# A mixture-of-experts stage on one core: experts ranked by row count, six of eight run with 96 rows as stationary tiles, eleven weight slots

## The reference

```
def moe_ffn(x, w_router, wg, wu, wd):
    logits = (xf @ w_router)
    top_v, top_i = lax.top_k(logits, 2)
    top_w = softmax(top_v)
    combine = sum(one_hot(top_i, 8) * top_w[..., None], axis=1)
    for e in range(8):
        out = out + combine[:, e:e + 1] * (silu(xf @ wg[e]) * (xf @ wu[e])) @ wd[e]
```

## Time and profile before

| | us |
|---|---|
| three runs | 1996.62, 1998.37, 1999.4 (median 1998.37) |
| profiled execution, its own time | 2003.87 |
| span of the program within it | 2002.0 |
| PE busy / DVE / ACT / POOL | 1873.6 / 375.4 / 248.8 / 137.8 |
| MoE loop, first gate matmul to the copy of the last result | 1030.64 to 1975.71 |

### The profile page before, as it was taken

How to read it: one execution, slowest core, us unless ns; L and a number is a source line. 1 busy time by engine, 2 the same in 40 slices (tenths; PEclk the granted TensorE clock), 3 DMA queues, 4 the chain that set the end, 5 groups by cost and what they waited for, 6 DMA issues and landing times.

```text
span 2002.0 us, 36594 instructions
## 1 busy us (share of the span) xinstructions
PE 1873.6 (94%) x15695; PEld 1515.0 (76%) x15695; DVE 375.4 (19%) x823; ACT 248.8 (12%) x539; POOL 137.8 (7%) x198
## 2 busy tenths in 40 slices
PE   6699999899999999898879999999999999999994
PEld 5489997677776886665679597896969879596982
DVE  2798012100003016564210000000000000000002
ACT  1001001100000115544020000000000000000001
POOL 2053000300000011231010000000000000000001
PEclk9799999899998999999979999999999999999997
DMA  9844655673563626787449799898979989797994
GB/s 243 227 146 147 202 187 203 245 280 126 188 253 127 142 78 266 248 287 221 132 143 296 262 344 300 289 316 273 335 260 343 304 285 321 269 338 262 337 308 150
DMA packets 354325, 484.74 MB, mean 242 GB/s; under 512 B 32612, under 2 KB 311150, under 8 KB 353580
## 3 DMA queue, kind: packets, MB, share of 16 engines
q1 hardware_dynamic: 325600, 392.40, 61.5%
q10 hardware_dynamic: 15500, 45.66, 6.9%
q0 software_dynamic: 13120, 45.15, 6.4%
HBM read 450.51 MB, written 40.98 MB: 245 GB/s over the span
## 4 chain that ended last, share of the span: by engine, by line
issue 49%; PE 44%; ACT 2%; DVE 2%; another core or an unknown queue 1%; DMA 1%; ACTq 1%; POOL 0%; SPq 0%; POOLq 0%; DVEq 0%
PE ps L1414 15%; PE ps L1444 8%; PE ps L1538 4%; PE ps L1560 2%; PE ps L1725 2%; PE ps L1583 2%; PE ps L1644 1%; PE ps L1736 1%; PE ps L1792 1%; PE ps L1382 1%; PE ps L1640 1%; ACT arena L887 1%; PE ps L1675 1%; PE ps L1657 1%
## 5 line engine op out<-in xcount | busy, mean ns | idle before, releaser
L1874 PEld LDWEIGHTS ps<-arena 128*128 128x128 f32 x5632 | 632.9, 192 | 5.1 <-issue 5.0
L1874 PE MATMUL ps<-arena 128*128 128x128 f32 x5632 | 633.2, 275 | 1.3 <-ACT arena L922 1.3
L1414 PE MATMUL ps<-arena 128*128 128x288 f32 x1216 | 304.3, 414 | 23.6 <-DMA arena<-in_conv_w_pw 18.5
L1884 PE MATMUL ps<-arena 128*128 128x512 f32 x704 | 304.2, 593 | 1.7 <-DVE arena L1326 1.7
L1414 PEld LDWEIGHTS ps<-arena 128*128 128x128 f32 x1216 | 235.7, 194 | 91.6 <-DMA arena<-in_conv_w_pw 19.0
L1884 PEld LDWEIGHTS ps<-arena 128*128 128x128 f32 x704 | 133.1, 190 | 168.1 <-issue 168.1
L1326 DVE TENSOR_TENSOR arena<-arena,ps 128x256 f32<-128x256 f32 x88 | 37.0, 421 | 883.9 <-ACT arena L938 883.9
L1444 PE MATMUL ps<-arena 64*64 64x128 f32 x4096 | 160.4, 312 | 6.9 <-issue 6.9
L1444 PEld LDWEIGHTS ps<-arena 64*64 64x64 f32 x4096 | 156.0, 248 | 11.1 <-issue 10.4
L1030 DVE SCALAR_TENSOR_TENSOR arena<-arena 128x256 f32<-128x256 f32 x240 | 119.9, 588 | 0.0
L938 ACT ACTIVATE arena<-ps 128x256 f32<-128x256 f32 x88 | 33.7, 383 | 531.2 <-PE ps L1874 531.1
(11 more groups left out here) (308 smaller groups left out, 1045.5 us busy)
## 6 DMA issues: line engine op xcount, KB each, us to landing
arena<-in_moe_w_gate SPq DMA_DIRECT2D x88, 1024.0 KB, 6.7
arena<-in_moe_w_up SPq DMA_DIRECT2D x88, 1024.0 KB, 7.2
arena<-in_moe_w_down SPq DMA_DIRECT2D x88, 1024.0 KB, 5.0
arena<-in_cache_kv SPq DMA_DIRECT2D x176, 256.0 KB, 5.3
arena<-in_cache_kv POOLq DMA_DIRECT2D x80, 256.0 KB, 7.3
xg_scratch<-arena POOLq DMA_DIRECT2D x26, 512.0 KB, 17.7
arena<-in_conv_w_pw SPq DMA_DIRECT2D x12, 1024.0 KB, 14.6
arena<-in_cmp_w ACTq DMA_DIRECT2D x6, 2048.0 KB, 22.2
```

The costliest lines, as they stand in the source:

```text
L1414: ins = mm(dst, w[:, k, c * P:(c + 1) * P], rhs[:, k, :], start=(k == 0), stop=(k == KD - 1))
L1874: ins = mm(dst, w[:, k, c * P:(c + 1) * P], XeT[:, k, :], start=(k == 0), stop=(k == KD - 1))
L1884: ins = mm(ps[:, 4 + c, :], He[:, 2 * k + kk, :], w[:, kk, 512 * c:512 * (c + 1)], start=(k == 0 and kk == 0), stop=(k == 10 and kk == 1))
```

## The change

DVE ranks the experts by row count. The two largest get places 0 and 4 in the loop and room for 128 rows, as before; the six others get places 1, 2, 3, 5, 6, 7 and room for 96 rows (`CAP`), with the overflow rows and the flag made to match. An expert's scratch rows go by its place, and SyncE reads the expert of a place from `orderI`. In the six, the roles of the operands are swapped: 32 rows of `XeT` are the stationary operand, and the weights stream. Four such matmuls stand next to each other in the source, each writing another 32 partitions of `ps`: the first two 32-row groups with gate and with up (256 columns each), and for the third group the same in the last pass of two units together. The products are now row by row, so PE transposes them back (`columns_out`), ScalarE copies them into `HT`, and the down projection streams 256 columns of weights past 32 stationary columns of `HT`, four quarters of the output next to each other, for three row groups. The ring gets six more slots (`MRING` = 11) in memory that the attention no longer needs; SyncE waits for the whole ring to be free and for the order before it loads the first expert. Six more stores of zeros stand on ScalarE's queue behind the 16 of L773, and an expert's result is stored in three pieces.

```
-EPAD = 35
+EPAD = 33
+MRING = 11
+CAP = P - 32
...
             for b in range(NE, 3 * NE):
                 act.dma_start(yg_dram[b * P:(b + 1) * P, :], zero).then_inc(sem("y_put"), 16)
+            for b in (1, 2, 3, 5, 6, 7):
+                act.dma_start(yg_dram[b * P + CAP:(b + 1) * P, :], zero[0:P - CAP]).then_inc(sem("y_put"), 16)
...
-            def experts(e, turn):
+            def experts(j, turn):
+                e = sp.value_load(orderI[0:1, bass.ds(j, 1)], min_val=0, max_val=NE - 1)
                 for k in range(33):
-                    sp.wait_ge(slot_used, turn * EPAD + (M0 + k - RING + 1))
-                    slot = ring[:, k % RING, :]
+                    last = k - MRING
+                    sp.wait_ge(slot_used, turn * EPAD + (M0 + (4 * (last // 4) + 4 if 0 <= last < 20 else last + 1)))
+                    slot = mslots[k % MRING]
...
+            sp.wait_ge(slot_used, M0)
+            sp.wait_ge(sem("rid_ready"), 2)
...
+            def fewer(n, turn):
+                def columns_in(u):
+                    c0, c1 = HCOL[u]
+                    act.wait_ge(sem("ht_mm"), n * 11 + (u + 1))
+                    sc.activation(HT[:, c0:c1], ps[:, 7, 64:64 + c1 - c0], ACT.Copy).then_inc(sem("ht_ev"), 1)
...
+                for u in range(11):
+                    if u:
+                        columns_in(u - 1)
+                    act.wait_ge(slot_used, turn * EPAD + (M0 + (2 * u + 2 if u % 2 or u == 10 else 2 * u + 1)))
+                    act.wait_ge(sem("gu_ev"), turn * 11 + (u + 1))
+                    sc.activation(es[64:, u % 2, 0:HROW[u]], ps[0:64, 2 + u % 2, 0:HROW[u]], ACT.Silu)\
...
+            def fewer(n, turn):
...
+                def columns_out(u):
+                    pe.wait_ge(sem("gu_ev"), turn * 11 + (u + 3))
+                    if u:
+                        pe.wait_ge(sem("ht_ev"), n * 11 + u)
+                    tr(ps[:, 7, 0:P], Hs[:, u % 2, 0:P], ident)
+                    for b in range(1, HROW[u] // P):
+                        ins = tr(ps[:, 7, 64 + 64 * b:2 * 64 + 64 * b], Hs[64:, u % 2, b * P:(b + 1) * P], ident[64:, 64:])
+                    ins.then_inc(sem("ht_mm"), 1)
...
+                for u in range(11):
...
+                    for k in range(KD):
+                        for j in range(4):
+                            m, g = divmod(j, 2)
+                            ins = mm(ps[quarter(j), bk, 0:2 * P], XeT[:, k, quarter(g)], pair[m][:, k, :], start=(k == 0),
+                                     stop=(k == KD - 1), skip_group_check=True)
...
+                    if u:
+                        columns_out(u - 1)
...
+                    elif u % 2:
+                        for k in range(KD):
+                            for j in range(4):
+                                m, r = divmod(j, 2)
+                                ins = mm(ps[quarter(j), bk, 2 * P:4 * P], XeT[:, k, quarter(2)], (held, pair)[r][m][:, k, :],
...
+                for k in range(11):
+                    if k == 1:
+                        columns_out(10)
...
+                    for kk in range(2):
+                        for g in range(3):
+                            for j in range(4):
+                                ins = mm(ps[quarter(j), 4 + g, 0:256], rows(g, k, kk),
+                                         w[:, kk, 256 * j:256 * (j + 1)], start=(k == 0 and kk == 0), stop=(k == 10 and kk == 1),
...
+            with pe.Fori(0, 2, 1) as h:
+                experts(h * 4)
+                with pe.Fori(0, 3, 1) as s:
+                    fewer(h * 3 + s, h * 4 + (s + 1))
```

More of the change, by code:

```diff
@@ L332, in build @@
         rkB = take(3, NE, NE)
+        HT = He.rearrange("p a b -> p (a b)")
+        key8 = take(NE)
+        rank8 = take(NE)
+        place = take(2, NE)
+        cap8 = take(NE)
+        room8 = take(NE)
+        sort8 = take(NE, NE)
+        order8 = take(NE)
+        orderI = base0[0:1, cursor[0]:cursor[0] + NE].bitcast(I32)
+        cursor[0] += NE
         flag = base0[:, cursor[0]:cursor[0] + 1].bitcast(I32)
@@ L337, in build @@
         sqM = take(KD, T)
+        sqflat = sqM.rearrange("p a b -> p (a b)")
+        Hs = sqflat[:, 0:8 * P].rearrange("p (a c) -> p a c", a=2)
+        es = sqflat[:, 8 * P:16 * P].rearrange("p (a c) -> p a c", a=2)
+        gsflat = Gs.rearrange("p t j d -> p (t j d)")
+        mslots = [ring[:, s, :] for s in range(RING)] + [view(KV0 + i * SLOT, SLOT) for i in range(4)] \
+            + [gsflat[:, i * SLOT:(i + 1) * SLOT] for i in range(2)]
+        assert len(mslots) == MRING and KV0 + 4 * SLOT <= SMALL0
         top_moe = cursor[0]
@@ L400, in build @@
             need.append((s, counts[s]))
-        per = [len(range(s, 33, RING)) for s in range(RING)]
+        mfull = [(full[s], counts[s]) for s in range(RING)] + [(sem(f"kv_in{u}"), (PAIRS - 1) * (64 if u < 8 else 32))
+                                                              for u in range(0, 10, 2)] + [(sem("kv_first0"), 4 * 64 + 32)]
         M0 = -(-NPRE // RING) * RING
@@ L407, in build @@
         slot_used = sem("slot_used")
+        HROW = [(4 if u % 2 else 3 if u == 10 else 2) * P for u in range(11)]
+        HCOL = [(384 * (u // 2) + 128 * (u % 2), 384 * (u // 2) + 128 * (u % 2) + HROW[u] // 2) for u in range(11)]
         class Link:
@@ L1308, in _ @@
             v.tensor_copy(ridI, rid.rearrange("p t j -> p (t j)")).then_inc(sem("rid_ready"), 1)
+            row = place[0:1, 1]
+            link(v.tensor_tensor(sort8[0:1], row.unsqueeze(1).to_broadcast([1, NE, NE]),
+                                 erow[0:1].unsqueeze(2).to_broadcast([1, NE, NE]), ALU.is_equal))
+            link(v.tensor_tensor(sort8[0:1], sort8[0:1], erow[0:1].unsqueeze(1).to_broadcast([1, NE, NE]), ALU.mult))
+            link(v.tensor_reduce(order8[0:1], sort8[0:1], AXX, ALU.add))
+            v.tensor_scalar(orderI, order8[0:1], 1.0 / P, None, ALU.mult).then_inc(sem("rid_ready"), 1)
             dve.wait_ge(sem("rt_exp"), 1)
@@ L1328, in experts @@
                      .then_inc(sem("gu_ev"), 1)
-            with dve.Fori(0, NE, 1) as e:
-                experts(e, e)
+            link(v.memset(Hs[0:64], 0.0))
+            def fewer(n, turn):
+                for u in range(11):
+                    dve.wait_ge(sem("gu_exp"), turn * 11 + (u + 1))
+                    if u >= 2:
+                        dve.wait_ge(sem("ht_mm"), n * 11 + (u - 1))
+                    v.tensor_tensor(Hs[64:, u % 2, 0:HROW[u]], es[64:, u % 2, 0:HROW[u]], ps[64:, 2 + u % 2, 0:HROW[u]],
+                                    ALU.mult).then_inc(sem("gu_ev"), 1)
+            with dve.Fori(0, 2, 1) as h:
+                experts(h, h * 4)
+                with dve.Fori(0, 3, 1) as s:
+                    fewer(h * 3 + s, h * 4 + (s + 1))
             dve.wait_ge(sem("flag_ready"), 1)
@@ L1858, in rows_in, with eslot @@
                 ins.then_inc(sem("xt_mm"), 1)
+            def eslot(turn, k):
+                filled, first = mfull[k % MRING]
+                pe.wait_ge(filled, turn * 48 + (first + 16 * (k // MRING + 1)))
+                return mslots[k % MRING]
             def experts(turn):
[L1861 to L1864, removed]
                 pe.wait_ge(sem("xe_ev"), turn + 1)
```

108 lines of the change are left out of this document (86 added, 22 removed).

## The result

The changed kernel takes 1928.36 us (median of four runs, 1925.55 to 1930.78); the kernel before, beside it, 1997.95 (1996.62 to 1999.40). The ratio is 0.9651, 95% interval 0.9634 to 0.9668: faster by 70 us, where 133 were forecast, and outside the range on the slow side. The profiled execution took 1927.19 us, its span is 1925.5.

The account below looks back on a forecast made before the run. PE was taken to bound the MoE loop, busy 938 of 942 us. Six small experts at 94.7 instead of 118.1 us (-140.4), start +7.1 and end +0.5 sum to -132.8: 1998.4 to 1866 us, range 1848 to 1908.

Parts of the forecast that it names:

- PE waits for nothing: MoE loop of the kernel before: PE busy 938 of 942 us, 118.1 us an expert, so PE sets the pace.
- The last sentence of the prediction: If waits break up PE's work and its clock falls to 1.2 GHz, tiled passes double there and the time is higher.
- A four of 256 columns, 215 ns: Small experts on PE: one instruction on each of four column tiles takes 215 ns together; 388 of these an expert.
- rivals 3 and 4: Column tiles overlap incompletely or share a limit: a four costs 314 or 288 ns, 2101 or 2036 us; chance 0.03 each.
- Transposes and changes of shape: Small experts on PE: 41 transposes at 0.108 us, 4.4 us, and 35 tile-shape changes at 0.15, 5.2 us.
- Rival 2: A four costs 225 ns, or transposes wait half a microsecond in each of eleven units; 1890 us, chance 0.15.
- A small expert, 94.7 us: PE's time for each of the six experts in the new form, 94.7 us against 118.1 before.
- The weights keep up: Weight loads at 348 GB/s for gate and up, 410 for down, take 96.8 us an expert with rows; none comes late.
- Rival 1: The weights become the bound of the MoE loop; 1877 us with 348 GB/s throughout, 1918 with 324 and 333; chance 0.18.
- The start, +7.1 us: Start of the MoE stage: 2.6 us for DVE's routing, 2.4 for the scatter, 2.1 for the rows' load.
- The end, +0.5 us: End of the stage: ScalarE copies three quarters of what took 1.02 us and issues two more DMAs at 0.36.
- whether the flag stays down: Rival that a third expert has over 96 rows, raising the flag and adding sixteen turns of 118 us; 3750, chance 0.01.

Follow-up runs that it names:

- e1: The changed kernel with the eight expert turns written out in TensorE's program, no loop, other engines keeping theirs; 1869.32 us, ratio 0.9342.
- e5: The changed kernel with only the inner loop over the three small turns written out in TensorE's program, one jump back left; 1880.77 us, ratio 0.9402.
- e2: The changed kernel with its loops, SyncE loading only a quarter of each weight slot from the second turn on; 1890.28 us (one run).
- e7: The changed kernel with eight useless 512-column matmuls (16 instructions) added on TensorE behind each small turn, ahead of the jump; 1927.90 us (one run).
- e3: The kernel before with two experts in each pass of TensorE's loop, four passes in place of eight, same work; 2000.84 us, ratio 1.0013.
- e10: e1 with SyncE waiting for the scatter of the tokens before it loads the first weight slot; 1864.48 us, ratio 0.9328.
- e4: The changed kernel with its ranking, order and eleven slots, but all eight experts in the form for 128 rows; 2012.86 us, ratio 1.0075.

## Why the prediction was wrong

**The step that failed** is the sentence "PE waits for nothing", carried from the kernel before to the new one. The sum had a term for every instruction that PE gets, but none for bringing those instructions to it. From the first gate matmul to the last down matmul the changed kernel takes 859.7 us (1035.6 to 1895.3), and written out 804.4 (1039.2 to 1843.6). The forecast's own terms give 2 x 118.1 + 6 x 94.7 = 804.4. The 55.3 us between are the five jumps: 38.7 us idle (32.9 + 5.8 in the groups), and 16.6 us of slower matmuls at half clock. For these the two groups of the written-out kernel stand against 254.3 and 162.8:

```profile
L2016 PE MATMUL ps<-arena 128*32 128x256 f32 x4224 | 240.4, 379 | 0.7 <-DMA arena<-in_moe_w_up 0.4
L1967 PE MATMUL ps<-arena 128*128 128x128 f32 x1408 | 160.1, 277 | 1.1 <-ACT arena L951 1.1
```

e1 and e5 show that the jumps cause this, e2 and e7 why it is as large as it is. The last sentence of the prediction named half clock behind waits of PE as what would put it wrong upwards; that PE would wait for its own instructions it did not see.

The trace of before held what was needed: 1600 instructions in a turn from the counts of the earlier trace rows, 3314 in the new one from the source, and six blocks fetched in the first turn only. The Trainium skill's page "Runtime: NRT & Kernel Launch", section Instruction fetch mechanics, says that prefetch is sequential and that a jump to instructions that aren't held stalls for a fetch. I had not weighed it. The seams of the changed kernel and of e1 agree with it, with 5.92 us and none; e3 and e7 add that its first part can be covered. The same section gives TensorE 128 KiB of instruction memory, 2048 instructions, and then says that this memory is only two lines of 16 KiB. Here a loop of 1600 instructions, six blocks, ran seven more turns without a fetch, and one of some 3300 is fetched anew: for TensorE that agrees with the first figure and decides against the second.

Term by term, from e1 where the jumps don't blur it:

- **A four of 256 columns, 215 ns**: 216. Right; rivals 3 and 4 (272 ns and more) fall.
- **Transposes and changes of shape**: a pair of units takes 11.74 us (1299.79 to 1311.53), 192 instructions of 54.0 ns are 10.37, six transposes 0.65; the rest is 0.12 us for each of six changes, where 0.15 was taken. No transpose waits for DVE. Rival 2 falls.
- **A small expert, 94.7 us**: turns start 94.2 us apart (1253.65, 1347.81). Right.
- **The weights keep up**: 349 GB/s over 799 us and 0.4 us of waits. Right; rival 1 falls. In the changed kernel PE waits for no weight slot either.
- **The start, +7.1 us**: from the routing's copy to the first gate matmul it was 19.84 us and is 30.35, +10.5. DVE's part is 2.5 (2.6 forecast). The scatter is 4.8 later, where I took 2.4 between bounds of 0 and 6, and the rows' load 3.2, where I took 2.1. Mis-sized by 3.4 us; e10 shows the cause that was named, weights in flight. That the gate came near the forecast 1038 (1035.6) is chance, because what lies ahead of the routing ran 5.5 us sooner (1005.25, before 1010.80).
- **The end, +0.5 us**: mis-sized. From ACT's last copy to the end of the span it is 30.05 us, before 26.3. The timeline of the changed kernel shows where:

```profile
1895.45 0.81 ACT L997 ACTIVATE arena<-ps 128x768 f32<-128x768 f32 x1 [25.83 <-PE ps L2049]
1896.43 2.03 ACTq L1000 DMA_DIRECT2D yg_scratch<-arena  x3
1903.39 0.98 POOL L658 DMA_INDIRECT arena<-yg_scratch,arena  x1 [884.47 <-ACTq L1017]
```

  Three stores take 2.03 us to issue, where 0.36 each were counted for two more, and the gather follows 4.9 us behind; the single store of before was issued in 0.36 us and the gather followed 2.7 us behind. With three stores of whole rows in e4 the gather follows 2.4 us behind. That points at the 1 KB pieces in which a small expert's rows are stored; no run changes these alone.

In the span: 2002.0 - 5.5 (ahead of the routing) + 10.5 - 85.2 (the loop up to ACT's last copy, from 945.1 to 859.9) + 3.7 = 1925.5. Of the missing 56 us (1925.5 against 1869), the jumps are 55.3, start and end 6.6, and the earlier routing takes 5.5 back.

The chances were right in sign (faster 0.93). The range was too narrow because no rival had PE's own program in it: they asked whether the work is as fast as counted, whether the data arrive, and whether the flag stays down.

## What to carry to other kernels

A change that makes a loop's work shorter in time but longer in instructions moves the loop towards its instruction supply: count the instructions of the body, and look at the packets of the instruction queue in the trace to see whether the body stays on the chip. Where it doesn't, the jump back is a stall. Long instructions ahead of it covered its first part (e3, e7), DMA engines with little to do about halved it (e2), and writing the turns out removed it here at no cost that shows. And when a prefetch is moved behind a dependency, look at what then shares the DMA engines with the transfers that the dependency itself waits for.

## What the runs showed of the hardware

A jump back of TensorE to instructions that had to be fetched cost 11.1 us on the mean of five in the changed kernel, with the DMA engines full: 5.7 to 5.9 us to the first instruction, at four of the five a second stall of 2.2 to 2.6 us until the next block was there, and a granted clock of 0.50 in stretches behind the gaps. With the DMA engines at 0.22 the two gaps of a seam were 3.3 and 1.4 us and the clock stayed at 1.00. The sequencer runs at least seven matmuls ahead of the array: in e7 the block behind the jump was on its way from 1251.11, when 3.0 of the 7.14 us of long matmuls, seven of them, were still to come. And useless work was free: sixteen long matmuls ahead of each jump left the time as it was (one run).

Open is how long a body TensorE holds (some 1600 instructions stay, some 3300 don't), and why the second block sets out only 4.8 to 5.1 us after the first has arrived (2.1 to 2.6 with a quarter of the weights).
